# A second block's output projection, cut so that more of it can run inside the attention loop

## The reference

```python
h = rmsnorm_2(x, norm_mix_w)
z = h @ w_in
u, v, q, k_c, v_c, k_s, v_s, k_w, v_w, g_raw = jnp.split(z, offsets, axis=-1)
a = gmlp_group(u, v, gmlp_norm_w, gmlp_ws, gmlp_bs)      # gelu(u) * (W_s rmsnorm(gelu(v)) + b), 512 channels
b = nsa_group(q, k_c, v_c, ...)                          # sliding and compressed attention, 512 channels
mix = jnp.concatenate([rmsnorm_2(a, out_norm_a_w), rmsnorm_2(b, out_norm_b_w)], axis=-1)
x = x + mix @ w_o
h = rmsnorm_2(x, norm_ffn_w)
x = x + (jax.nn.silu(h @ w_gate) * (h @ w_up)) @ w_down
```

## Time and profile before

| | us |
|---|---|
| median of three runs | 2559.98 |
| the profiled execution | 2559.84 |
| its span | 2557.7 |
| mean granted TensorE clock | 0.996 |
| TensorE busy | 2518.2 (98%) |
| vector engine busy | 1315.8 (51%) |
| ScalarE busy | 566.9 (22%) |
| GpSimd busy | 1519.2 (59%) |

### The profile page before, as it was taken

One profiled execution on the slowest core, in us unless ns is written; L12 is line 12 of the kernel. 1 busy time (PEld: TensorE's weight loads), 2 busy tenths in 40 slices (PEclk: granted clock), 3 DMA queues, 4 the chain that ended last, 5 costly groups with the idle time before them and its releaser, 6 DMA issues.

```text
span 2557.7 us, 33017 instructions
## 1 busy us (share of the span) xinstructions
PE 2518.2 (98%) x11986; PEld 2058.2 (80%) x11986; DVE 1315.8 (51%) x1556; ACT 566.9 (22%) x1033; POOL 1519.2 (59%) x858
## 2 busy tenths in 40 slices
PE   8999999999999999999999999999999988999998
PEld 6888888778888888888888778888887776888887
DVE  5555527656555315556137656555226656655522
ACT  2110014652111001110015552111013564111000
POOL 5666666436666666666665536666664322666664
PEclk9999999999999999999999999999999999999999
DMA  4233222113222322332322112332233111332232
GB/s 166 96 98 98 94 96 75 58 42 98 93 96 98 99 93 97 98 95 93 99 96 69 56 50 93 98 121 93 98 99 132 57 35 34 99 96 93 99 99 74
DMA packets 66149, 228.67 MB, mean 89 GB/s; under 512 B 8721, under 2 KB 11665, under 8 KB 65681
## 3 DMA queue, kind: packets, MB, share of 16 engines
q1 hardware_dynamic: 64352, 225.67, 27.1%
q10 hardware_dynamic: 1712, 1.82, 0.2%
HBM read 225.36 MB, written 2.10 MB: 89 GB/s over the span
## 4 chain that ended last, share of the span: by engine, by line
PE 96%; DVE 2%; ACT 1%; POOL 1%; issue 1%; DMA 0%; SPq 0%; DVEq 0%; POOLq 0%; ACTq 0%
PE bank L606 28%; PE bank L608 28%; PE bank L607 28%; PE bank L623 2%; PE bank L755 2%; PE bank L740 2%; PE bank L724 1%; PE bank L629 1%; PE bank L725 1%; PE bank L978 1%; PE bank L993 1%; DMA raw<-in_stream 0%; POOL wl L570 0%; PE bank L614 0%; PE bank L970 0%
## 5 line engine op out<-in xcount | busy, mean ns | idle before, releaser
L570 POOL TENSOR_TENSOR wl<-raw,wh 128x1024 fp32r<-128x1024 f32 x412 | 1035.7, 2514 | 34.5
L567 POOL TENSOR_SCALAR wh<-raw 128x1024 fp32r<-128x1024 f32 x412 | 445.5, 1081 | 985.8 <-PE bank L608 947.8
L606 PE MATMUL bank<-xh,wh 128*128 128x512 f32 x2096 | 818.8, 391 | 0.2 <-POOL wl L570 0.2
L607 PE MATMUL bank<-xl,wh 128*128 128x512 f32 x2096 | 816.4, 389 | 0.0
L608 PE MATMUL bank<-xh,wl 128*128 128x512 f32 x2096 | 816.2, 389 | 0.0
L608 PEld LDWEIGHTS bank<-xh,wl 128*128 128x128 f32 x2096 | 393.5, 188 | 83.0
L607 PEld LDWEIGHTS bank<-xl,wh 128*128 128x128 f32 x2096 | 393.6, 188 | 81.4 <-issue 0.2
L606 PEld LDWEIGHTS bank<-xh,wh 128*128 128x128 f32 x2096 | 393.7, 188 | 81.1 <-POOL wl L570 0.6
L606 PE MATMUL bank<-acth,wh 128*128 128x512 f32 (+1 forms) x902 | 346.4, 384 | 0.0
L607 PE MATMUL bank<-actl,wh 128*128 128x512 f32 (+1 forms) x902 | 346.2, 384 | 0.0
L608 PE MATMUL bank<-acth,wl 128*128 128x512 f32 (+1 forms) x902 | 346.2, 384 | 0.0
(11 more groups left out here) (269 smaller groups left out, 2344.0 us busy)
## 6 DMA issues: line engine op xcount, KB each, us to landing
raw<-in_stream SPq DMA_DIRECT2D x412, 512.0 KB, 3.7
x<-in_x SPq DMA_DIRECT2D x4, 512.0 KB, 7.9
w1k<-in_w1k SPq DMA_DIRECT2D x1, 2048.0 KB, 9.0
w1v_low<-in_w1v SPq DMA_DIRECT2D x1, 1024.0 KB, 6.8
w1v_high<-in_w1v SPq DMA_DIRECT2D x1, 1024.0 KB, 10.0
out_dram<-x SPq DMA_DIRECT2D x4, 256.0 KB, 2.6
out_dram<-x SPq DMA_DIRECT2D x1, 768.0 KB, 3.7
invcount<-in_c_invcount ACTq DMA_DIRECT2D x1, 512.0 KB, 6.1
```

Of the source, the lines that this page charges most:

```text
L567: nc.gpsimd.tensor_scalar(wh[:, h, :, :], src, 1.0, 1.0, ALU.mult, ALU.mult)\
L570: nc.gpsimd.tensor_tensor(wl[:, h, :, :], src, wh[:, h, :, :].bitcast(F32), ALU.subtract).then_inc(split_done, 1)
L606: mm = nc.tensor.matmul(bank, wh[:, slot, k, :], rh, start=start, stop=False)
L607: mm = nc.tensor.matmul(bank, wh[:, slot, k, :], rl, start=False, stop=False)
```

## The change

All of it is in the second block.

- The output projection is cut into four units of gated halves (tiles (6,7), (0,1), (2,3), (4,5)) and four of attention halves ((0,1), (2,3), (4,5), (6,7)).
- The gated halves of tiles 6 and 7 go to banks 0 and 1 and are added to x by the vector engine in the loop (`gated_part`, steps 57 and 59); then tiles 0 and 1 use these banks. Their attention halves go to banks 7 and 6 and are added with the ordinary updates.
- Blocks stand at steps 54 to 57 (two each) and 60 to 63 (1, 2, 1, 1), then 5, instead of one in each of 56 to 63.
- The last input units are used one step sooner (2, 3, 3 blocks at steps 41 to 43 instead of 1, 1, 3, 3 at 41 to 44).
- The gating's steps are moved: scaling 39 to 38, `spatial_out` 41..44 to 40..43, `gated` 45, 46 to 44, 45, sums 49 to 48, rows 52 to 50, `normed` 53, 54 to 50, 51, high and low parts three steps sooner. Of the compressed attention, scores and bias of pair 2 move from 44 and 45 to 38 and 39, the second minimum from 49 to 50, its exponential from 50 to 51, its normalisation from 51 to 53, its turn from 54 to 55, the copy from 55 to 56, the output from 56 to 57.

```diff
-FILL2 = tuple(2 + (G in (9, 12, 15, 18, 21, 24, 27, 29, 31, 33, 35, 37, 39, 40)) if G < 41 else (1, 1, 3, 3)[G - 41]
-              if G < 45 else 0 for G in range(STEPS2))
+FILL2 = tuple(2 + (G in (9, 12, 15, 18, 21, 24, 27, 29, 31, 33, 35, 37, 39, 40)) if G < 41 else (2, 3, 3)[G - 41]
+              if G < 44 else 0 for G in range(STEPS2))
+OUT_BANKS = ((0, 1), (0, 1), (2, 5), (3, 4), (0, 1), (2, 5), (3, 4), (7, 6))
 OUT_BANK = (0, 1, 2, 5, 3, 4, 7, 6)
+OUT_FILL = {54: (0, 2), 55: (2, 4), 56: (4, 6), 57: (6, 8), 60: (8, 9), 61: (9, 11), 62: (11, 12), 63: (12, 13)}
...
             def out_half(unit, js):
                 uo = u0 + U_PROJ2
+                banks = OUT_BANKS[unit]
                 for j in js:
-                    m, k = 2 * (unit % 3) + j // 4, 4 * (unit // 3) + j % 4
-                    if unit >= 6:
-                        m, k = unit, j
+                    k = 4 * (unit // 4) + j % 4
                     if j == 0:
                         pe.wait_ge(split_done, uo + unit + 1)
+                    if unit == 1 and j % 4 == 0:
+                        pe.wait_ge(part_x, j // 4 + 1)
                     pe.wait_ge(ml2_done, k + 1)
...
-                if G in (22, 24, 44, 48):
-                    compressed_scores((22, 24, 44, 48).index(G))
-                if G in (30, 54):
+                if G in (22, 24, 38, 48):
+                    compressed_scores((22, 24, 38, 48).index(G))
+                if G in (30, 55):
                     compressed_turn(G // 32)
...
-                if G == 49:
+                if G == 48:
                     pe.wait_ge(asum, 3)
                     pe.wait_ge(evac2, EVACUATED[GU_UNIT[3]])
                     token_sums(0, B[1], gv[:, 0, :], True, True).then_inc(ss2_done, 1)
-                if G == 52:
+                if G == 50:
                     pe.wait_ge(rstd2_done, 1)
                     norm_rows(B[1]).then_inc(rows_done, 1)
-                if G >= 56:
-                    out_half(0, [G - 56])
+                if G in OUT_FILL:
+                    for j in range(*OUT_FILL[G]):
+                        out_half(j // 8, [j % 8])
...
             turn2(STEPS2 - 3)
+            out_half(1, range(5, 7))
             turn2(STEPS2 - 2)
+            out_half(1, range(7, 8))
             pe.wait_ge(t2_done, STEPS2 + 2)
-            out_half(1, range(2))
+            out_half(2, range(2))
...
+            def gated_part(m):
+                if m == 6:
+                    dve.wait_ge(x_done, 8 * 8)
+                    dve.wait_ge(gated_tiles, 1)
+                else:
+                    dve.wait_ge(unit_used, u0 + U_PROJ2 + 3)
+                V.scalar_tensor_tensor(x[:, m, :], B[m - 6][:, :], 1.0, x[:, m, :], ALU.mult, ALU.add).then_inc(part_x, 1)
...
...
                 if G == 38:
                     dve.wait_ge(gsq_done, NQ)
                     V.tensor_scalar(gss[:, :], gss[:, :], 1.0 / 512, EPS, ALU.mult, ALU.add).then_inc(gv_mean, 1)
-                if G == 39:
                     dve.wait_ge(gv_root, 1)
                     V.reciprocal(gss[:, :], gss[:, :]).then_inc(gv_rstd, 1)
...
-                if G == 50:
+                if G == 48:
                     dve.wait_ge(ss2_done, 1)
                     token_means(0, B[1][:, 0:NQ], mean2)
...
+                if G in (57, 59):
+                    gated_part(6 + G // 59)
```

More of the change, by code:

```diff
@@ L1025, in out_half @@
                 uo = u0 + U_PROJ2
+                banks = OUT_BANKS[unit]
                 for j in js:
-                    m, k = 2 * (unit % 3) + j // 4, 4 * (unit // 3) + j % 4
-                    if unit >= 6:
-                        m, k = unit, j
+                    k = 4 * (unit // 4) + j % 4
                     if j == 0:
                         pe.wait_ge(split_done, uo + unit + 1)
+                    if unit == 1 and j % 4 == 0:
+                        pe.wait_ge(part_x, j // 4 + 1)
                     pe.wait_ge(ml2_done, k + 1)
-                    mm = split_product(B[OUT_BANK[m]][:, :], unit % 2, j, mh2[:, k, :], ml2[:, k, :], k == 0, k == KT - 1)
-                    if j == 7:
+                    mm = split_product(B[banks[j // 4]][:, :], unit % 2, j, mh2[:, k, :], ml2[:, k, :],
+                                       k == 0 or (unit == 7 and k == 4), k == KT - 1 or (unit == 0 and k == 3))
+                    if j == 3 and unit == 0:
+                        mm.then_inc(gated_tiles, 1)
+                    elif j == 7:
                         mm.then_inc(unit_used, 1)
@@ L1104, in _ @@
             mm.then_inc(shared_written, 1)
-            out_half(2, range(3))
+            out_half(3, range(3))
             pe.wait_ge(rstd2_done, 2)
@@ L1108, in _ @@
             norm_rows(shared).then_inc(shared_written, 1)
-            out_half(2, range(3, 8))
-            for unit in range(3, 8):
-                if unit == 6:
+            out_half(3, range(3, 8))
+            for unit in range(4, 8):
+                if unit == 7:
                     claim("norm_rows")
@@ L2108, in _ @@
                     evacuate2(GV_UNIT[2], gv[:, 2, :])
-                if G in (23, 25, 45, 49):
-                    compressed_bias((23, 25, 45, 49).index(G))
-                if G in (25, 49):
-                    compressed_minimum(G // 32)
-                if G in (28, 51):
+                if G in (23, 25, 39, 49):
+                    compressed_bias((23, 25, 39, 49).index(G))
+                if G == 25:
+                    compressed_minimum(0)
+                if G in (28, 53):
                     compressed_normalise(G // 32)
@@ L2125, in _ @@
                     V.tensor_scalar(gss[:, :], gss[:, :], 1.0 / 512, EPS, ALU.mult, ALU.add).then_inc(gv_mean, 1)
-                if G == 39:
                     dve.wait_ge(gv_root, 1)
                     V.reciprocal(gss[:, :], gss[:, :]).then_inc(gv_rstd, 1)
-                if 41 <= G < 45:
-                    spatial_out(G - 41)
-                if G == 43:
+                if 40 <= G < 44:
+                    spatial_out(G - 40)
+                if G == 42:
                     add_b(1)
-                if G in (45, 46):
-                    gated(2 * G - 90)
-                    gated(2 * G - 89)
+                if G in (44, 45):
+                    gated(2 * G - 88)
+                    gated(2 * G - 87)
+                if G == 46:
+                    add_a(1)
                 if G == 47:
-                    add_a(1)
-                if G == 48:
                     add_a(2)
                     add_a(3)
-                if G == 50:
+                if G == 48:
                     dve.wait_ge(ss2_done, 1)
                     token_means(0, B[1][:, 0:NQ], mean2)
-                if G == 51:
+                if G == 49:
                     token_inverse(0)
-                if G in (53, 54):
+                if G == 50:
+                    compressed_minimum(1)
+                if G in (50, 51):
                     dve.wait_ge(rows_done, 1)
-                    normed(0, 2 * G - 106, B[1][:, :]).then_inc(norm_mul, 1)
-                    normed(0, 2 * G - 105, B[1][:, :]).then_inc(norm_mul, 1)
-                if G in (55, 56):
-                    low_mix(2 * G - 110)
-                    low_mix(2 * G - 109)
+                    normed(0, 2 * G - 100, B[1][:, :]).then_inc(norm_mul, 1)
+                    normed(0, 2 * G - 99, B[1][:, :]).then_inc(norm_mul, 1)
+                if G in (52, 53):
+                    low_mix(2 * G - 104)
+                    low_mix(2 * G - 103)
+                if G in (57, 59):
+                    gated_part(6 + G // 59)
                 if G == 59:
@@ L2243, in lay_out @@
     out_units = [cols(a["w_o_2"][0], m * P) for m in range(KT)]
-    units += [np.concatenate([out_units[m][:, k:k + 4], out_units[m + 1][:, k:k + 4]], 1)
-              for k in (0, 4) for m in range(0, 6, 2)] + out_units[6:]
+    for k, firsts in ((0, (6, 0, 2, 4)), (4, (0, 2, 4, 6))):
+        units += [np.concatenate([out_units[m][:, k:k + 4], out_units[m + 1][:, k:k + 4]], 1) for m in firsts]
     ffn(a["w_gate_2"][0], a["w_up_2"][0], a["w_down_2"][0])
```

50 lines of the change are left out of this document (25 added, 25 removed).

## The result

The changed kernel takes 2565.01 us (median of 16 runs, 2562.93 to 2567.08); the kernel before, on the same chips, 2559.61 us (16 runs, 2558.25 to 2562.46). The ratio is 1.002 with an interval of 1.0014 to 1.0027: slower by 5.4 us. Forecast were 2554.8 us, and 2565.0 is outside the range of 2549.5 to 2560.5. The profiled execution took 2565.32 us with a span of 2563.2, 5.5 more than before.

The account below looks back on a forecast made before the run. TensorE, busy 98% of the span, was taken as the bound, so only its idle stretches could give time. The terms -3.1 - 1.3 + 0.8 + 1.2 - 2.6 summed to -5.0 us, giving 2554.8 us, range 2549.5 to 2560.5.

Parts of the forecast that it names:

- Steps 44 to 53: Second block's loop, where the vector engine sets the pace: 23.7 us against 25.0, so -1.3 us, between -3.3 and +2.5.
- TensorE is two steps ahead here: At step 48, TensorE's lead was to keep small the vector engine's wait for token sums made in the same step.
- over 2 us of vector idle: Sign that the forecast is wrong: the vector engine idle over 2 us at steps 38 or 48.
- Rival (a): The loop gives nothing: new waits at steps 38, 48 or 50 take the gain of 40 to 44; 2558.3 us, chance 0.17.
- Steps 40 to 44: Second block's loop up to the scores of step 44: waits and half clock go, other work moves ahead; -3.1 us.
- all three waits: Waits of spatial(0) for gvtok (2.42 us), spatial(1) (1.76) and spatial(2) (0.39) for svt, taken as gone: 4.6 us.
- the half clock behind spatial(0): TensorE's slow clock at spatial(0) and three instructions behind it, taken to go with the wait: 1.6 us, 0 to 1.6.
- Steps 54 to 57: Eight blocks in four steps instead of two: 10.0 us against 9.2 to the scores of step 58, +0.8 us.
- 58 to the last turn: End of the loop, ten blocks instead of eight: +1.2 us, between 0 and +2.0.
- rival (d): Slower: half clock reaches over the blocks of steps 54 to 59, +11 us there; 2565.8 us, chance 0.10.
- The addition that the forecast had named: add_b(2) may meet a GpSimd split at step 58 or 59: up to 2.2 us longer, the sum 0 or +1 us.
- The tail: Behind the last turn: 8 blocks fewer save 5.4 us, a new 2.9 us wait for tile 7; -2.6 us, 0 to -5.4.

Follow-up runs that it names:

- E3: The changed kernel with ScalarE's copy of turn 43 moved ahead of high_q2(3) and two squares at step 45: 2563.52 us, ratio 1.0006 to the kernel before.
- E6: The changed kernel with E3's and E4's edits, group 0's normalisation back at its old steps, blocks of 54 to 57 at 56 to 59: 2555.67 us, 0.9980.
- E4: The changed kernel with the vector engine's update of tile 7 ahead of the sum of squares of tile 5: 2560.96 us, ratio 0.9999 to the kernel before.
- E7: The changed kernel with E3's and E4's edits and scores and bias of pair 2 back at steps 44 and 45: 2557.90 us, 0.9992.
- E8: The kernel before with the change's projection cut and E4's edit, no gating step moved: 2559.29 us, 0.9997.
- E2: The kernel before with only the change's projection (units, blocks, banks, gated_part), gating steps unmoved: 2563.85 us, 1.0008.
- E1: The kernel before with all moved steps of gating and compressed attention, but its own output projection: 2563.29 us, 1.0009.
- E10: The changed kernel unaltered, profiled once more: 2566.47 us in its one run.
- E12: The kernel before with the gating of E6 alone, keeping its own projection and order of updates: 2556.77 us, 0.9986.
- E9: E6 with the blocks of the projection's unit 4 reordered, so the low parts that come last are asked for last: 2553.20 us, 0.9974.
- E11: E9 with E7's edit, scores and bias of pair 2 back at steps 44 and 45: 2553.60 us, 0.9971.

## Why the prediction was wrong

**The step that failed: "Steps 44 to 53", -1.3 us, measured +3.7.** Its busy time was right (21.7 us forecast, 21.59 measured from score row to score row), its idle time was not: 2.0 forecast, 7.1 measured, where it was 5.8 before. The vector engine's timeline of the changed kernel shows the longest of it, in waits for TensorE and ScalarE:

```profile
2100.22 0.69 DVE L2078 CUSTOM_DVE_ANT_0 sq<-bank,tri 128x512 f32<-128x512 f32 x1 [1.74 <-PE bank L974]
...
2102.02 0.16 DVE L2024 TENSOR_SCALAR rs<-bank 128x4 f32<-128x4 f32 x1 [1.10 <-PE bank L1020]
...
2111.40 0.56 DVE L2078 CUSTOM_DVE_ANT_0 sq<-bank,tri 128x384 f32<-128x384 f32 x1 [1.23 <-PE bank L974]
2113.09 1.29 DVE L2040 TENSOR_TENSOR ml<-mixed,mh 128x512 fp32r<-128x512 f32 x2 [1.13 <-ACT mh L1440]
```

The forecast let the waits of before go (2.50 and 1.32 us) and took new ones to be small because "TensorE is two steps ahead here". TensorE was not: it waited 3.49 us in step 47 for a copy of ScalarE's, then at half clock, and had lost its lead when step 48 asked for the token sums. ScalarE's queue was never walked through. In the kernel before, `high_q2(3)` and the first two squares stand in step 46, behind the copy of turn 43 that opens it. The change moves both to step 45 (its list above does not name them), and with that 2.4 us (1.28 and 1.15) go ahead of the copy. The chain sums, mean, root, reciprocal, rows then ran step upon step, each link a full trip between engines, and the root stood behind a copy, an exponential and its own table load:

```profile
2103.62 1.28 ACT L1436 ACT_TABLE_LOAD   x1
2104.91 0.21 ACT L1436 ACTIVATE rs<-rs 128x4 f32<-128x4 f32 x1
```

E3 (2.0 us at the last turn, 1.4 to 2.6 in the time) and E6 (1.85, and 2.9 in the time) change one of the two each, and together they give back 4.1 of the 4.6 (with E4's edit, which lies behind). The copy's share is shown by one moved instruction; E6 moves work as well as the chain, so its share is shown for the place of both, not for the trips alone. The prediction had named the place (step 48, "over 2 us of vector idle") and an upper end of +2.5; it took the low one by an argument on the wrong engine. The vector engine was idle 1.74 and 1.10 us in step 48, so its own sign of being wrong was there. Rival (a) had the mechanism, with the price at 3.5 us for the whole loop; the last turn came 7.0 later than forecast.

**Steps 40 to 44: -3.1, measured -0.6.** The waits for svt at spatial(1) and (2) went, with the half clock behind spatial(0). The 2.42 us ahead of spatial(0) did not: it had a second end. Once gvtok was early, the same instruction waited 1.48 for the last reader of the shared bank, and the compressed output one turn ahead of it 0.88 for the bias of pair 2 in the same bank, together 2.36 us. The bias itself stood behind the new wait for ScalarE's root at step 38, 1.15 us, which the forecast had taken at nothing. That "all three waits" are gone was read from the one releaser that each row of before names. E7 shows the part of pair 2: with its scores and bias back, the 0.88 us and the 1.0 of scores leave this stretch. The 1.6 us for the half clock behind spatial(0) were no fixed price either: behind the same wait of 2.42 us the product took 1.97 us before and 1.09 in E8.

**Steps 54 to 57, +0.8 (measured +1.0), and 58 to the last turn, +1.2 (+0.6).** Right. The clock there is 1.00, so rival (d), which ended at 2565.8 us, met the measured time with a mechanism that did not occur. The addition that the forecast had named, `add_b(2)`, did meet the split (2129.35 to 2131.72), but only its last part: 1.19 us instead of 0.7, so neither nothing nor the 2.2 us more.

```profile
2131.08 1.19 DVE L2021 TENSOR_TENSOR graw<-graw,vs 128x512 f32<-128x512 f32 x1 [0.92 <-ACT vs L1428]
```


**The tail, -2.6, measured +0.9.** The mechanism was right and its largest term too: 2.9 us of new wait forecast, 2.81 measured, at L627, the line that was L623. Missing was the half clock behind two waits: 1.7 us behind that for the low parts (2165 to 2172) and 1.6 behind that for xh (E4). -5.4 + 2.8 + 1.7 + 1.6 = 0.7; 0.2 stay open. E2, which has the wait for xh but not the first of the two episodes, bears out the 1.7: its tail is 50.9 us against 52.6. The low-part waits, 0.49 and 1.81 us, were priced right and stayed, but the clock behind them changed.

Of the 10.5 us between forecast and measurement some 5.0 lie in steps 44 to 53, 3.5 in the tail (3.3 of them half clock) and 2.5 in steps 40 to 44; the two stretches behind step 54 give 0.4 back. That the loop's loss comes with the moves is settled by E1, E3 and E6; the arithmetic on the blocks of steps 54 to 57 held.

## What to carry to other kernels

When a step moves, walk the queue of every engine that it touches in the new step, and ask what stands ahead of the items that TensorE waits for: a 0.26 us copy behind 2.4 us of work not yet needed cost some 2 us, and one line's place gave it back. A wait has more than one end: before counting it as gone, find who last touched the same bank or buffer, since the row names only the later of them. A shorter stretch of matmuls in front of an updates chain exposes the chain, so bring forward what TensorE asks for first there (the last tile's update, before a sum of squares) in the same change.

## What the runs showed of the hardware

A wait of 1.8 or 2.8 us was followed by some 3 us at half clock, with TensorE fully busy. The changed kernel by stretches, and then the kernel before at its own low-part wait (length, busy, granted clock, DMA share, GB/s):

```profile
2161.00:2165.00 4.00, 1.70 (x7) 1.00 0.00 0
2165.00:2168.00 3.00, 3.00 (x8) 0.53 0.55 183
2168.00:2172.00 4.00, 4.00 (x17) 0.93 0.00 0
```

```profile
2157.00:2160.00 3.00, 0.98 (x3) 1.00 0.00 0
2160.00:2163.00 3.00, 2.75 (x12) 1.00 0.52 178
```

The waits are alike (0.49 and 1.8 us), so is the transfer beside them, and yet 0.53 stands against 1.00. The changed kernel, E3 to E8 and E10 have the half clock there, and the kernel before, E1, E2 and E12 do not. But it is not settled by the kernel's instructions alone: E2 and E8 differ only in the order of the updates behind this wait, and behind the same 1.80 us E2 kept full clock and E8 did not. E2, then E8, three microseconds of each:

```profile
2165.00:2168.00 3.00, 3.00 (x14) 1.00 0.54 175
```

```profile
2163.50:2166.50 3.00, 3.00 (x10) 0.69 0.55 180
```

What makes the difference was not found. Behind the wait of 2.8 us for xh the clock fell in all four profiles that have this wait (the changed kernel, E10, E2 and E3). So the 1.7 us behind the low-part wait are no fixed price of the instructions, while the fall behind the wait for xh came each time. In E9 and E11, with one wait of 1.25 us, the clock stays up; that its shorter wait is the reason is argued, not shown.
